# Router and experts in one block, the last gate tiles moved there, and gather and memory quarter ahead of an expert's products

## The reference, cut to what matters

```python
mod = jax.nn.silu(c) @ w_ada[l] + b_ada[l]
sh1, sc1, g1, sh2, sc2, g2 = jnp.split(mod, 6, axis=-1)
...
y = jnp.concatenate([attn.astype(x.dtype), hm], axis=-1) @ w_out[l]
x = x + g1[:, None, :] * y
h2 = modulate(x, norm2_g[l], sh2, sc2)
moe = hier_moe(h2.reshape(b * s, d), w_rg[l], b_rg[l], w_re[l], b_re[l],
               w1[l], w3[l], w2[l]).reshape(b, s, d)      # top group of 4, top 2 of its 8 experts
x = x + g2[:, None, :] * moe
return rms_norm(x, norm_f_g)
...
ys = (jax.nn.silu(xb @ w1[e]) * (xb @ w3[e])) @ w2[e]     # per expert e of 32, on its tokens
...
k, v = jnp.split(mem_n @ w_kv, 2, axis=-1)                # second network: memory keys and values
```

## Time and profile before

| what | value |
|---|---|
| median of three runs | 1487.52 us (1485.95 to 1488.42) |
| profiled execution, its own time | 1488.37 us |
| its span, first to last instruction | 1486.6 us |
| mean granted TensorE clock | 0.96 of full speed |
| TensorE busy | 1375.4 us (93%) |
| bytes read from memory | 379.76 MB |
| DMA share and rate, 260 to 700 us | 1.01, 426 GB/s |
| DMA share and rate, 740 to 1486 us | 0.43, 155 GB/s |
| TensorE busy, 740 to 1486 us | 724.28 of 746 us |

### The profile page before, as it was taken

One profiled execution on the slowest core, in us unless ns is written; L12 is line 12 of the kernel. 1 busy time (PEld: TensorE's weight loads), 2 busy tenths in 40 slices (PEclk: granted clock), 3 DMA queues, 4 the chain that ended last, 5 costly groups with the idle time before them and its releaser, 6 DMA issues. The chain is left out here.

```text
span 1486.6 us, 24369 instructions
## 1 busy us (share of the span) xinstructions
PE 1375.4 (93%) x10107; PEld 1039.3 (70%) x10107; DVE 656.5 (44%) x1235; ACT 267.3 (18%) x573; POOL 228.3 (15%) x227
## 2 busy tenths in 40 slices
PE   5999988997888877888899999999999999999998
PEld 2476546775665655565468688888887877788887
DVE  2445533111010110111544326385299999986563
ACT  2222111121011100011111032100233333230000
POOL 0000100000000000000365640099222112000000
PEclk9999997999899998798999999999999999999999
DMA  9755758999999999999633434456663444334440
GB/s 399 305 234 217 302 217 331 427 425 426 424 425 427 423 428 426 423 426 427 252 153 113 150 133 151 161 191 227 211 214 111 165 159 157 130 119 164 160 171 37
DMA packets 50828, 388.22 MB, mean 261 GB/s; under 512 B 6289, under 2 KB 21393, under 8 KB 29089
## 3 DMA queue, kind: packets, MB, share of 16 engines
q1 hardware_dynamic: 48128, 381.35, 64.1%
q10 hardware_dynamic: 2592, 5.31, 1.0%
HBM read 379.76 MB, written 6.88 MB: 260 GB/s over the span
## 5 line engine op out<-in xcount | busy, mean ns | idle before, releaser
L2569 PE MATMUL ps<-hT,ring 128*128 128x256 f32 x768 | 171.2, 383 | 1.0 <-PEq L2009 1.0
L2569 PEld LDWEIGHTS ps<-hT,ring 128*128 128x128 f32 x768 | 146.4, 193 | 21.0 <-issue 1.3
L1470 DVE TENSOR_TENSOR ada_part<-ada_part,ps 64x256 f32<-64x256 f32 x32 | 13.5, 423 | 256.7 <-ACT ada_part L1426 256.7
L1538 POOL TENSOR_SCALAR end_stat<-end_ss 128x1 f32<-128x1 f32 x2 | 0.9, 472 | 500.1 <-ACT expert L1528 500.0
L1057 PEld LDWEIGHTS ps<-sel,tokens 128*128 128x128 f32 x544 | 72.5, 217 | 6.9 <-issue 6.5
L1342 PE MATMUL ps<-memT,hT 128*128 128x256 f32 x192 | 55.2, 451 | 22.8 <-DMA hT<-in_mem_quarters 22.8
L1057 PE MATMUL ps<-sel,tokens 128*128 128x64 f32 x544 | 73.4, 301 | 1.6 <-DVE sel L1066 1.6
L1373 PE MATMUL ps<-ring,x_gathered 128*32 128x256 f32 x736 | 51.2, 428 | 23.2 <-DMA ring<-in_experts 18.3
L267 PE MATMUL ps<-ring,hT 128*128 128x512 f32 x160 | 69.8, 593 | 0.0
L1342 PEld LDWEIGHTS ps<-memT,hT 128*128 128x128 f32 x192 | 43.0, 229 | 35.6 <-DMA hT<-in_mem_quarters 26.1
L1858 PE MATMUL ps<-ring,zT 128*128 128x256 f32 x288 | 66.8, 379 | 0.0
(11 more groups left out here) (653 smaller groups left out, 2561.9 us busy)
## 6 DMA issues: line engine op xcount, KB each, us to landing
ring<-in_weights SPq DMA_DIRECT2D x69, 2048.0 KB, 7.8
expert<-in_experts SPq DMA_DIRECT2D x36, 2048.0 KB, 29.8
ring<-in_experts SPq DMA_DIRECT2D x35, 2048.0 KB, 29.6
expert_room<-in_experts SPq DMA_DIRECT2D x12, 2048.0 KB, 28.7
late_room<-in_experts SPq DMA_DIRECT2D x12, 2048.0 KB, 29.7
hT<-in_mem_quarters SPq DMA_DIRECT2D x20, 512.0 KB, 26.9
s_c_bar<-c_bar_out ACTq DMA_DIRECT2D x16, 256.0 KB, 2.1
c_bar<-s_c_bar SPq DMA_DIRECT2D x16, 256.0 KB, 2.7
```

The lines of the kernel that those rows point to most:

```text
L1470: dve.tensor_tensor(act_s, gate, h_ps[w3_out, :], ALU.mult).then_inc(act_ready, 1)
L2569: last = pe.matmul(out[:, f, :], w[:, kk, (2 * h + f) * P:(2 * h + f + 1) * P], k.hT[:, kk, :], start=(kk == 0), stop=(kk == KD - 1))
```

## The change

The two gate tiles A10 and A11 leave the mixing block; router and experts become one block, whose programs come from `route_programs` with one function for each engine. In the mixing block A9 goes behind the output products, the two halves of the contraction are interleaved otherwise, and all logits are computed there, in four pieces as the modulated halves become ready. In the loop the gather and the memory quarter stand ahead of an expert's first two products. Two rooms of expert tiles swap, and each engine waits for the number of passes before it loads it.

The diff, cut to its core:

```diff
-         "VM", "OM", "A6", "A7", "A8", "A9", "O0", "O1", "A10", "A11", "M2")
+         "VM", "OM", "A6", "A7", "A8", "O0", "O1", "A9", "A10", "A11", "M2")
...
@@ stage_mix, sync
-                    if n == TILE_OF["O0"]:
+                    if n == TILE_OF["O1"]:
                         ...
                         load_expert_tile(k, sp, a, 3)
-                    if n == TILE_OF["A10"]:
+                    if n == TILE_OF["A9"]:
                         sp.wait_ge(squares, 2)
                         load_expert_tile(k, sp, a, 4)
@@ stage_mix, tensor
                 ada_columns(k, banks, pe, 8, part)
-                ada_tile(k, banks, pe, 9, crep)
                 pe.wait_ge(mixT_ready, 1)
-                for n in range(N_OUT):
-                    for t in range(TT):
-                        out_half(0, t, n)
-                ada_columns(k, banks, pe, 9, part)
+                for t in range(TT):
+                    out_half(0, t, 0)
                 turn_mix(1)
+                for t in range(TT):
+                    out_half(0, t, 1)
                 pe.wait_ge(mixT_ready, 2)
...
                 turn_x(0)
-                ada_tile(k, banks, pe, 10, crep)
-                ada_row(k, banks, pe, 10, part)
+                ada_tile(k, banks, pe, 9, crep)
+                ada_columns(k, banks, pe, 9, part)
                 turn_x(1)
-                pe.wait_ge(h_first_ready, 2)
-                logits_of(k, a, pe, 0)
+                for t in range(TT):
+                    for half, ready in enumerate((h_by_dve, h_by_act)):
+                        pe.wait_ge(ready, t + 1)
+                        ...  # four of the eight products of token tile t
+                last.then_inc(a["logits_done"], 1)
@@ stage_mix, scalar, behind the four squares
-                act.wait_ge(x1_turned, 1)
-                act_modulate(k, a, act, 0).then_inc(h_first_ready, 1)
-                take_part(10)
+                take_part(9)
+                act.wait_ge(gain_ready, 1)
+                for t in range(TT):
+                    act.wait_ge(x1_turned, t + 1)
+                    act_modulate(k, a, act, t).then_inc(h_by_act, 1)
@@ stage_mix, vector
-                dve_modulate(k, a, dve, 0).then_inc(h_first_ready, 1)
+                dve_modulate(k, a, dve, 0).then_inc(h_by_dve, 1)
                 scale_x(1)
-                take_row(10, k.row("b_g2")[:, 0:512])
+                take_columns(9, 28)
+                gains(4).then_inc(gain_ready, 1)
+                dve.wait_ge(x1_turned, 2)
+                dve_modulate(k, a, dve, 1).then_inc(h_by_dve, 1)
@@ route_programs (was stage_route)
+    def sync(sp):
+        load_expert_tile(k, sp, a, 5)
+        load_expert_tile(k, sp, a, 7)
+        sp.wait_ge(k.tile_done, TILE_OF["A10"] + 1)
+        load_expert_tile(k, sp, a, 8)
+        sp.wait_ge(h_turned, TT)
+        load_part(k, sp, a, 1)
+        sp.wait_ge(k.tile_done, TILE_OF["A11"] + 1)
+        load_expert_tile(k, sp, a, 6)
+        load_part(k, sp, a, 8)
...
+    def tensor(pe):
+        turn_back(0)
+        pe.wait_ge(logits_copied, 1)
+        ...  # two transposes of the logits
+        ada_tile(k, banks, pe, 10, a["crep"])
+        turn_back(1)
+        ada_row(k, banks, pe, 10, a["part"])
+        ada_tile(k, banks, pe, 11, a["crep"])
+        pe.wait_ge(chosen_ready, 1)
+        ...  # five products of the ranks
+        ada_row(k, banks, pe, 11, a["part"])
+        pe.wait_ge(h_copied, TT)
+        pe.wait_ge(first_sel_ready, 1)
+        gather(k, a, pe)
+        ...  # four products with zeros that open the sums, from stage_experts
...
+    def vector(dve):
+        ...  # the chain as before, with take_row(10) behind chosen_ready and take_row(11) at the end
@@ stage_experts
         def passes(eng):
+            eng.wait_ge(a["passes_ready"], 1)
             return eng.value_load(a["passes"][0:1, 0:1], min_val=1, max_val=MAX_PASS)
...
-                for n, last in ((T_END_FIRST, 88), (T_END_FIRST + 1, 93), (T_END_FIRST + 2, 94)):
+                for n, last in ((T_END_FIRST, 88), (T_END_FIRST + 1, 94), (T_END_FIRST + 2, 93)):
...
                         if b == 0:
                             pe.wait_ge(xg_ready, p * N_PAIR + (i * 4 + (q + 1)))
+                        else:
+                            pe.wait_ge(sel_ready, s + 2)
+                            gather(k, a, pe)
+                        if parts[b] is not None:
+                            pe.wait_ge(y_ready, s + 1)
+                            memory_part(p, i, q, b, parts[b])
                         pe.wait_ge(act_ready, s + 1)
                         for j in range(2):
                             ...  # products with tiles 3e and 3e+1
-                        if parts[b] is not None:
-                            pe.wait_ge(y_ready, s + 1)
-                            memory_part(p, i, q, b, parts[b])
-                        pe.wait_ge(sel_ready, s + 1 + b)
-                        if b == 1:
-                            gather(k, a, pe)
+                        if b == 0:
+                            pe.wait_ge(sel_ready, s + 1)
                         pe.wait_ge(y_ready, s + 1)
                         turn_selection(b)
```

More of the change, by code:

```diff
@@ L31 @@
 ROUND = 12582912.0
-FRONT = ("A0", "A2", "A1", "A3", "Q", "K", "V", "U0", "A4", "U1", "A5", "VM", "OM", "A6", "A7", "A8", "A9",
-         "O0", "O1", "A10", "A11", "M2")
+FRONT = ("A0", "A2", "A1", "A3", "Q", "K", "V", "U0", "A4", "U1", "A5", "VM", "OM", "A6", "A7", "A8", "O0", "O1",
+         "A9", "A10", "A11", "M2")
 TILE_OF = {name: n for n, name in enumerate(FRONT)}
@@ L222, with __init__ @@
 class TwoBanks:
-    def __init__(self, k, name, pieces):
-        self.k, self.pieces = k, [p.split(":") for p in pieces.split()]
+    def __init__(self, k, name, pieces, first=0):
+        self.k, self.pieces, self.first = k, [p.split(":") for p in pieces.split()], first
         self.at = {p: i for i, (p, _owner) in enumerate(self.pieces)}
@@ L235, in bank @@
     def bank(self, p):
-        return self.k.ps[:, 6 + self.at[p] % 2, :]
+        return self.k.ps[:, 6 + (self.first + self.at[p]) % 2, :]
     def out(self, p):
@@ L368, in stage_mix @@
          o_part, gcol_ready, ops_out, x1_added, x1_summed, x1_rstd_ready, x1_scaled, x1_turned,
[L369 removed]
+         h_by_dve, h_by_act, gain_ready) = (k.sem(n) for n in names)
         fm = lambda b0, n: k.ps[:, b0:b0 + n, :].rearrange("p b (f t) -> p (b f) t", f=2)
@@ L586, in _ @@
                 turn_x(0)
-                ada_tile(k, banks, pe, 10, crep)
-                ada_row(k, banks, pe, 10, part)
+                ada_tile(k, banks, pe, 9, crep)
+                ada_columns(k, banks, pe, 9, part)
                 turn_x(1)
                 pe.wait_ge(a["w_router_in"], 16)
-                pe.wait_ge(h_first_ready, 2)
-                logits_of(k, a, pe, 0)
+                for t in range(TT):
+                    for half, ready in enumerate((h_by_dve, h_by_act)):
+                        pe.wait_ge(ready, t + 1)
+                        for kk in range(4 * half, 4 * half + 4):
+                            last = pe.matmul(a["by_expert_ps"][:, t * P:(t + 1) * P], a["w_router"][:, kk, :],
+                                             k.hT[:, kk, t * P:(t + 1) * P], start=(kk == 0), stop=(kk == KD - 1))
+                last.then_inc(a["logits_done"], 1)
             @block.scalar
@@ L966, in _, with gains @@
                 take_columns(8, 24)
+                def gains(f):
+                    dve.drain()
+                    g = k.mod[:, 24 + f:28 + f]
+                    return dve.scalar_tensor_tensor(out=g, in0=g, scalar=1.0, in1=k.col("norm2_g", f, 4), op0=ALU.add,
+                                                    op1=ALU.mult)
                 head_norm(1, 512, 128, slice(8, 12), o_m[:])
[L968 to L971, removed]
+                gains(0)
                 dve.wait_ge(mix_turned, 2)
@@ L1042, in load_part @@
     sp.dma_start(a["parts_w"][c % 2], k.dram["mem_quarters"][quarter_of(c)]).then_inc(a["parts_in"][c % 2], 16)
[L1045 to L1050, removed]
 def gather(k, a, pe):
@@ L1401, in _ @@
                 pe.sem_inc(done, DONE0)
-                for t in range(TT):
-                    for n in range(2):
-                        rows = slice(64 * n, 64 * n + 64)
-                        pe.matmul(k.ps[:, 2 * t + n, :], selT[rows, 1, 0:64].bitcast(BF16), y[rows, :].bitcast(BF16),
-                                  start=True, stop=False, skip_group_check=True)
                 pe.sem_inc(selT_done, 1)
@@ L1417, in _ @@
                     scatter(1, t, stop=True)
+            @block.gpsimd
+            def _(pool):
+                route_gpsimd(pool)
             @block.scalar
             def _(act):
+                route_scalar(act)
                 n_pass = passes(act)
```

303 lines of the change are left out of this document (144 added, 159 removed).

## The result

The changed kernel takes 1475.3 us in the median (1474.02 to 1477.84, 4 runs) against 1487.16 before (1485.95 to 1488.42, 4 runs): a ratio of 0.9922 with a 95% interval of 0.9907 to 0.9937, so 9.4 to 13.8 us less; 1476.6 was forecast. Run again beside later experiments, its ratio was 0.9937 (0.9923 to 0.9952). The profiled execution took 1474.02 us with a span of 1472.2, against 1488.37 and 1486.6.

What follows compares the result with a forecast made beforehand. From 259.0 us, when tile 10 starts, the experts' stage was taken as bound by its transfers and begun late; gains of 9.6 (loop start) and 1.3 (loop end), 10.9 off 1488.37, gave 1477.5, on the median's scale 1476.6 us; range 1472 to 1485.

Steps and rivals of the forecast that it cites:

- Mixing block: Out projection: second halves of the products start at 191.9 instead of 198.47 us, 6.6 us earlier.
- Logits: Router logits behind the output products: end at 215.6 instead of 224.62 us, 9.0 us earlier.
- Gate tiles and clock: A10 and A11 beside the router's chain: cost 0.5 us, keep TensorE at full clock, gather 3.7 instead of 7.06 us.
- Loading the passes: Ahead of the loop: loading the number of passes costs 0.9 us, bounds 0 and 1.2; loop starts 13.0 us earlier.
- Start of the loop: First expert pair: tile 11 moves from 254.3 instead of 263.9 us, gain 9.6, after a new 3.5 us transfer hole.
- End of the loop: Last expert: last product 5.0 us behind its second tile instead of 7.35, next block 9.9 against 11.25; gain 1.3.
- Half clock at the start: Rival, loop's head: clock falls by 226 us, tile 11 moves from 263.4, 1.8 us gain left, 1485.7 us; chance 0.14.
- Quarters that starve DMA: Rival, loop's pairs 4 to 7: transfer queue runs dry behind memory quarters, 24 us lost, 1501 us; chance 0.07.

Runs made afterwards that it cites:

- Experiment 4: Changed kernel with the two last gate tiles cut to one of eight products each and row sums to 32 of 512 columns; ratio 0.9961 to the kernel before.
- experiment 1: Changed kernel with the loop's old order (first 32 products ahead of gather and memory quarter), router and mixing block as changed; ratio 0.9939 to the kernel before.
- experiment 5: Changed kernel with the gather done three times over in pairs 4 to 7, same output; ratio 0.9936 to the kernel before.
- experiments 10: Changed kernel with the mixing block's second turn back behind the first halves of the out projection; 1479.11 us, ratio 0.9945 to the kernel before.

## Why the prediction was right, point by point

All differences are net of the 1.88 us.

- **Mixing block.** 6.6 us forecast; the second halves start 5.9 earlier (38.6 behind the products with `mix_const`, now 32.6). The first halves ran at a lower clock for part of 8.83 us (granted 0.53 from 174.35 to 178 us), which the sum did not have; the same kernel profiled again took 7.13 there, at 1.00.
- **Logits.** 9.0 forecast; they end at 214.0 for 224.62, 8.7 earlier.
- **Gate tiles and clock.** Full clock was taken; it is 1.00 from 195 to 340 us. Experiment 4 shows that the gate tiles keep it there. They were put at 0.5 us of their own, and cost nothing.
- **Loading the passes.** 0.9 was taken from bounds of 0 and 1.2. Nothing of it shows on TensorE: the zeros follow the gather at once, and the wait behind them is put down to VectorE's copy (0.70), within which a load could hide. On the path the low bound was right. The loop starts 13.75 us earlier, 13.0 forecast. The Trainium skill ("DMA: Bandwidth & Descriptors", section "Latency and other measured facts") gives a `tensor_load` a floor of about 0.6 us; no run here shows the load by itself.
- **Start of the loop.** The reorder's price was put at a gap of 3.5 us; the gap is 1.65, for the most part since tile 3 was done 1.4 earlier than worked out, net, of which 0.75 is the loop's earlier start. And the rule "a gap's length comes off the end", on which the sum rested, is too strong for a gap this short, by single traces: closing it brought 0.4 to 0.9. The gain here was 10.5 for 9.6.
- **End of the loop.** 5.0 and 9.9 behind the tile forecast, 4.96 and 9.78 measured; gain 1.47 for 1.3. The prediction let half clock in the second tile's products take this gain away; in the second profile they ran so (3.25), and the gain stayed. In experiment 1, with the old order, the same half clock cost 1.44 on top, so there the reorder is worth 2.9.
- **Missed.** 0.9 us behind the loop, where TensorE no longer waits 0.90 for VectorE between the two turns (0.34 in the second profile); and the gap at 212.5, worth about 2 us, which lay ahead of the stretch that was searched and was longer still in the kernel before, where nothing moved for four microseconds:

```profile
216.31:220.31 4.00, 3.65 (x26) 2.90 (x26) 0.89 (x2) 0.30 (x1) 0.00 (x0) 1.00 0.00 0
```

- **Rivals.** Half clock at the start became experiment 4, 4.7 us by the traces (5.8 and 3.6 by the two ratios), where 9.1 had been worked out for it. Quarters that starve DMA: the waits are there (24.9 us in 7), and 422 to 428 GB/s in each 20 us from 260 to 680 us; experiment 5 shows that they are slack.

The forecast of 10.9 us lies between 11.9 and 10.1, its two comparisons by medians; the profiled pair gave 12.5. The steps were off by up to 0.9 in both directions, so part of the nearness is luck. The turn's place and the gate tiles were taken out by themselves (experiments 10 and 4); the shares of the logits and of A9's new place are read from the traces alone.

## What to carry to other kernels

A stage that runs at the rate of its transfers is shortened ahead of its first full slice: look for every stretch below the flat rate between the last stage and this one, and ask for the next tile as soon as its room is free. Independent work put where an engine would wait for a short chain can pay twice, once for itself and once for the clock of what follows. An order that is good at one end of a loop can be bad at the other: here the same lines cost at the first pair and pay at the last.

## What was not expected of the hardware

In experiment 4 the clock fell behind 2.40 us of idleness, five short products and a short row sum (0.99 to 0.50), and 32 products of 64 columns in 7.06 us did not bring it back; the next 32, in 5.58 us, ended at full clock (0.81 in the window from 236 to 240 us). The same 16 products ran 8.83 us in one execution of the changed kernel and 7.13 in another, with the same instructions and the same wait of 1.06 ahead. The rate of one core's transfers stood at 422 to 428 GB/s in the changed kernel from 260 to 680 us.
